# Stick-breaking attention on one Trainium2 core: ScalarE's logarithm of a block put directly behind its exponential, ahead of an older block's weights

## The reference, cut to what matters

```python
def stick_breaking(q, k, v):
    ...
    for blk in range(S // SB_BLOCK):
        ...
        z = jnp.einsum('bthd,bshd->bhts', qf[:, q0:kend], kf[:, :kend]) * scale
        ...
        strict = s_idx < t_idx
        log_beta = jax.nn.log_sigmoid(z)
        log_one_minus = jnp.where(strict, jax.nn.log_sigmoid(-z), 0.0)
        suffix = lax.cumsum(log_one_minus, axis=3, reverse=True) - log_one_minus
        w = jnp.where(strict, jnp.exp(log_beta + suffix), 0.0)
        outs.append(jnp.einsum('bhts,bshd->bthd', w, vf[:, :kend]))
```

## Time and profile before

| | us |
|---|---|
| median of 3 runs | 2780.9 |
| lowest and highest run | 2776.28, 2781.06 |
| the profiled execution's own time | 2779.38 |
| its span, first to last instruction | 2777.6 |
| TensorE busy | 2571.7 (93% of the span) |
| VectorE busy | 1418.5 (51%) |
| ScalarE busy | 1153.7 (42%) |
| GpSimd busy | 378.4 (14%) |
| mean granted TensorE clock | 0.969 |
| the stick-breaking loops, from the first scores to the last product | 1934.4 to 2138.8 |

### The profile page before, as it was taken

One profiled execution on the slowest core, in us unless ns is written; L12 is line 12 of the kernel. 1 busy time (PEld: TensorE's weight loads), 2 busy tenths in 40 slices (PEclk: granted clock), 3 DMA queues, 4 the chain that ended last, 5 costly groups with the idle time before them and its releaser, 6 DMA issues. The chain is left out here.

```text
span 2777.6 us, 38801 instructions
## 1 busy us (share of the span) xinstructions
PE 2571.7 (93%) x14887; PEld 1986.1 (72%) x14887; DVE 1418.5 (51%) x2278; ACT 1153.7 (42%) x1977; POOL 378.4 (14%) x415
## 2 busy tenths in 40 slices
PE   5999999999999999879999999999998999999787
PEld 3778987877778978834337788786334877798776
DVE  5113265666655514666664723421777546265762
ACT  6112344545444321134443622311667647333662
POOL 1000020010020000046752000000000010004710
PEclk8999999999999999989999999999999999998889
DMA  7430000000112131200002220102000221111012
GB/s 265 165 139 23 18 33 1 1 1 1 62 61 91 39 61 46 49 19 1 1 1 91 92 76 31 44 18 76 1 1 23 81 89 32 38 46 61 1 54 76
DMA packets 87992, 139.74 MB, mean 50 GB/s; under 512 B 19513, under 2 KB 54738, under 8 KB 87682
## 3 DMA queue, kind: packets, MB, share of 16 engines
q1 hardware_dynamic: 70592, 75.90, 8.7%
q0 software_dynamic: 16976, 61.30, 6.1%
q10 hardware_dynamic: 242, 0.07, 0.0%
HBM read 120.47 MB, written 16.78 MB: 49 GB/s over the span
## 5 line engine op out<-in xcount | busy, mean ns | idle before, releaser
L169 ACT ACTIVATE WORK<-PS 128x512 f32<-128x512 f32 (+5 forms) x309 | 152.6, 494 | 660.3 <-PE PS L854 388.8
L854 PE MATMUL PS<-HT_R,W_R 128*128 128x512 f32 (+1 forms) x896 | 334.5, 373 | 0.0
L853 PE MATMUL PS<-WORK_R,W_R 128*128 128x512 f32 (+1 forms) x736 | 271.5, 369 | 0.0
L852 PE MATMUL PS<-WORK_R,W_R 128*128 128x512 f32 (+1 forms) x672 | 249.6, 371 | 14.4 <-DVE W_R L169 9.9
L980 PE MATMUL PS<-WORK_R,HT_R 128*128 128x512 f32 x528 | 210.5, 399 | 8.8 <-DVE W_R L169 7.5
L854 PE MATMUL PS<-W_R,WORK_R 128*128 128x256 f32 (+3 forms) x704 | 215.3, 306 | 0.0
L981 PE MATMUL PS<-WORK_R,MIXT_R 128*128 128x512 f32 x544 | 214.6, 394 | 0.0
L169 ACT ACTIVATE HT<-PS 128x1024 f32<-128x1024 f32 (+6 forms) x211 | 156.1, 740 | 135.0 <-PE PS L1288 99.3
L982 PE MATMUL PS<-W_R,HT_R 128*128 128x512 f32 x528 | 207.5, 393 | 0.0
L853 PE MATMUL PS<-W_R,HT_R 128*128 128x256 f32 (+2 forms) x688 | 206.2, 300 | 0.0
L917 PE MATMUL PS<-BASE,WORK 128*128 128x128 f32 (+1 forms) x1186 | 175.0, 283 | 23.7 <-DVE WORK L169 15.1
(11 more groups left out here) (330 smaller groups left out, 5607.2 us busy)
## 6 DMA issues: line engine op xcount, KB each, us to landing
MIXT<-in_w_mod POOLq DMA_DIRECT2D x8, 2048.0 KB, 8.8
x_scratch<-WORK POOLq DMA_DIRECT2D x24, 512.0 KB, 2.9
WORK<-x_scratch POOLq DMA_DIRECT2D x24, 512.0 KB, 3.5
W<-in_odd_w_in SPq DMA_DIRECT2D x12, 1024.0 KB, 5.1
W<-in_even_w_in SPq DMA_DIRECT2D x5, 2048.0 KB, 7.8
W<-in_w_mod SPq DMA_DIRECT2D x4, 2048.0 KB, 21.1
WORK<-in_x POOLq DMA_DIRECT2D x16, 512.0 KB, 8.2
W<-in_e_w_in SPq DMA_DIRECT2D x6, 1024.0 KB, 6.6
```

The lines of the kernel that those rows point to most:

```text
L169: self.last = Signalled(self, issue(*args, **kwargs))
L852: mm(out, a[0], b_[0], start=k == 0, stop=False)
L853: mm(out, a[1], b_[0], start=False, stop=False)
L854: return mm(out, a[0], b_[1], start=False, stop=k == KT - 1)
```

## The change

In ScalarE's loop, iteration n issued exponential n, weights n-2, logarithm n, decay n-2. It now issues exponential n, logarithm n, weights n-2, decay n-2. Nothing else is changed: no instruction, tile, semaphore or wait is added or removed.

```diff
@@ -2114,11 +2114,9 @@
                     e = SE[n % 2][:, :, 0:512 - cols_of(n)]
                     act.wait_ge(low_ready, n + 1)
                     f(e, e, ACT.Exp)
+                    f(e, e, ACT.Ln, bias=1.0).then_inc(ln_ready, 1)
                 if n >= 2:
                     stick_weights(n - 2)
-                if n < len(blocks):
-                    f(e, e, ACT.Ln, bias=1.0).then_inc(ln_ready, 1)
-                if n >= 2:
                     stick_decay(n - 2)
```

## The result

The changed kernel takes 2815.95 us (median of 4 runs, 2814.54 to 2816.87) against 2780.82 (4 runs, 2776.28 to 2781.06): ratio 1.0131, 95% interval 1.0115 to 1.0147, 35.1 us slower. That is the way and within the range forecast, 4.4 us above the 2811.6. The profiled execution took 2815.53 us.

What follows compares the result with a forecast made beforehand. A ring of hand-overs (weights, scores, cap, exponential, weights) bounds the stage. Three periods of 8.25 us make 24.75; with 5.10 ahead and 0.87 and 0.03 behind, about 30.7 us on 2780.9 gives 2811.6 us, range 2802 to 2825.

Steps and rivals of the forecast that it cites:

- The ring: Stick-breaking loops: weights, scores, cap, exponential, next weights wait in turn; the logarithm enters, a 12-block period grows 8.25 us.
- steps 12 and 14: Scores 12 to 13 and 14 to 15: logarithms of 0.66 and 0.45 us hidden wholly in slack under TensorE's own work.
- step 15: Scores 15 to 16: logarithm of 0.87 us, less 0.18 of slack at scores 16.
- step 10: Scores 10 to 11: an older add no longer delays the cap, 0.21 us off the logarithm's cost.
- step 17: Scores 17 to 18: an older add no longer delays the cap, 0.16 us off the logarithm's cost.
- step 18: Scores 18 to 19: an older add no longer delays the cap, 0.14 us off the logarithm's cost.
- step 19: Scores 19 to 20: a decay of 0.60 us leaves the exponential's way, logarithm adds 0.45; TensorE holds scores 20, no growth.
- The clock's case: Rival: TensorE's clock falls in the stage to 0.76, 10 to 59 us beyond the forecast, 2822 to 2870; chance 0.08.
- All logarithms exposed: Rival: slack at TensorE-held starts goes, so all 48 logarithms cost their length, 42 us, 2823; chance 0.04.
- Faster: Rival: logarithm fills ScalarE's wait for sums and the decay goes out earlier; 7.2 us at most, 2773.7; chance 0.03.
- no effect: Rival: the logarithm fits into ScalarE's 50.9 us of idle wherever it stands; chance 0.02.
- Half hidden: Rival: more steps are held by TensorE than modelled, growth only 8 to 20 us, 2795; chance 0.05.

Runs made afterwards that it cites:

- the changed kernel's second run: The changed kernel unaltered, timed again on the same chip as the kernel with fitted repeats: 2818.81 us, ratio 1.0144 to the kernel before.
- Experiment 1: Logarithm taken of the first head only: in the changed kernel 2804.12 us, ratio 1.0087; in the kernel before 2779.78 us, ratio 0.9998.
- experiment 2: Kernel before with weights first, exponential and logarithm side by side: decay last 2772.91 us, ratio 0.9977; decay right behind weights 2766.37 us, ratio 0.995.
- the last kernel of experiment 5: Changed kernel with values computed again in TensorE's idle pieces, without repeats that had not fitted: 2809.77 us, ratio 1.0109 to the kernel before.

## Why the prediction was right, and which term was short

**The ring, and the logarithm in it: shown.** A step with the clock up gives just what was worked out: +0.67 in the step above. A whole period with the clock up is in VectorE's timeline of the changed kernel's second run, caps 32 and 44:

```profile
2096.15 1.22 DVE L169 TENSOR_SCALAR HT<-PS 128x1024 f32<-128x1024 f32 x1 [0.41 <-PE PS L1504]
```

```profile
2154.62 1.23 DVE L169 TENSOR_SCALAR HT<-PS 128x1024 f32<-128x1024 f32 x1 [0.41 <-PE PS L1504]
```

58.47 us, where the forecast said 58.5; the same two caps of the kernel before are 50.32 apart, and the periods that the forecast was made for took 50.25. What the forecast took off for hidden parts was right to 0.1 us in each kind of step where the clock is up: steps 12 and 14 grew by nothing, step 15 by 0.68 (0.69 forecast), step 10 by 0.67 (0.66), step 17 by 0.50 (0.50), step 18 by 0.95 (0.95), and step 19 became 0.10 shorter (0 forecast). The one exception is step 17 in the first period, which grew by 0.79. Experiment 1 shows that the logarithm's own length is paid before the weights and not behind them, experiment 2 that the price goes when the weights stand first.

**Exponential and logarithm do not overlap.** 1.72 us for two of 0.84 in the changed kernel, 2.15 for two of 1.06 before. The Trainium skill's 93 ns of overlap ("ScalarE: Activation LUTs", What ACT_TABLE_LOAD costs) does not show in this in-place pair: each start is about 0.03 us behind the end before it. To go by the row was right.

**Softplus has no taker for an early logarithm:** in the loops no wait of VectorE for ScalarE appears, neither before nor after.

**The term that was missing** is the clock's, put at nothing by a step of that rival: "at the stage's own start TensorE was busy 3.64 of 7 us and the clock stayed at 1.00". I took that as evidence against a fall and left the clock out of the forecast. It was weak evidence: that stretch begins just behind one in which the kernel before did run low, a mean of 0.56 from 1934.39 to 1938.20. In the changed kernel the same stretch and the next one read:

```profile
1939.00:1946.00 7.00, 3.77 (x10) 1.31 (x10) 2.98 (x3) 4.49 (x5) 0.00 (x0) 0.83 0.21 66
1943.70:1950.50 6.80, 6.29 (x12) 2.11 (x14) 2.18 (x2) 2.70 (x4) 0.00 (x0) 0.50 0.00 0
```

The longer step 2 left TensorE idle for 2.64 us before scores 3, where it had been 1.55, and the clock went to its lower level, 1.2 GHz. It did so again in each of the three periods. The same idle pieces do not bring it down every time: in the kernel's second run the third period kept its clock. Here is the same kind of step twice, scores 12 to 13 and, a period later, 24 to 25, in TensorE's timeline of the changed kernel:

```profile
1993.84 1.56 PE L1513 MATMUL PS<-HT 128*128 128x384 f32 x4
1995.33 0.87 PE L1520 MATMUL PS<-HT,ONES 128*64 128x384 f32 x4
...
1996.98 1.13 PE L1504 MATMUL PS<-WORK 64*128 64x512 f32 x4
```

```profile
2052.55 2.61 PE L1513 MATMUL PS<-HT 128*128 128x384 f32 x4
2055.08 1.46 PE L1520 MATMUL PS<-HT,ONES 128*64 128x384 f32 x4
...
2057.33 1.13 PE L1504 MATMUL PS<-WORK 64*128 64x512 f32 x4
```

From 1992.99 the one took 3.99 us to the next scores; from 2051.70 the other took 5.63, with the clock at 0.50 from 2052.9 on. Scores 24 to 25 themselves took 3.98 us in the last kernel of experiment 5, the one with the fitted repeats, where the clock was up.

So the loops' 39.1 us are 30.7 forecast plus 8.4, and the 8.4 go with the low clock. Set beside that kernel, in which the clock stays up after the start, 6.5 us of it stand in five steps: 24 and 36 (1.64 each), 26 (1.52), 41 (0.96) and 10 (0.76). The rest, 1.9 us, is in step 3, which took 6.94 us where 4.21 and a logarithm of 0.87 make 5.08; it lies in the low stretch at the start, which the repeats do not reach.

Against it, 3.0 us came back outside the loops, which the forecast had put at nothing. About 1.5 of them lie behind the loops, where the clock's record has 6.8 us less at the lower level than in the kernel before (85.0 against 91.8). That end took 637.3 us in both runs of the changed kernel, each with 85.0 at the lower level, against 638.8. The other 1.5, ahead of the first cap, did not come again: the second run has its first cap at 1935.80, near the 1936.07 of the kernel before.

So it is partly luck that the whole kernel came within 4.4 us. The loops were 8.4 above their forecast, and the prediction's own sign for that was met: "if the clock in them is under 0.95 the size is wrong", and it was 0.94. The result lies in the upper part of the range, which had been drawn for all logarithms exposed and was filled by the clock. The clock's case had 0.08 and 10 to 59 us on top; it came true in part, with a mean of 0.94 and not 0.76, and cost less than its lower end.

**The rivals.** *All logarithms exposed* (42 us) fell, though the loops' 39.1 us come near it: scores 12 to 13, and the steps like it, still take 3.99 us where the clock is up, as in the kernel before. *Faster* and *no effect* fell with the sign. *Half hidden* fell: scores waited for the weights 42 times for 71.4 us. But the faster rival had its mechanism right for another order: once the weights are the first thing after the sums, ScalarE's wait is for the sums (34.4 us), and exponential, logarithm and decay have their place beside TensorE's work.

## What to carry to other kernels

An engine that idles a third of the time still has places where nothing is free: find the ring of hand-overs that releases the next buffer, and ask of each instruction whether it stands before or behind the hand-over on its engine. Work behind it was hidden here; the same work ahead of it cost its full length at every turn that no other engine held up. Putting the releasing instruction first, ahead of both the exponential and the logarithm, took 13 to 14 us off the kernel before, and 6.8 where a decay was left directly ahead of the next release. When a ring gets longer, count also what the bound engine's new idle pieces do to its clock.

## What the runs showed of the hardware

- A granted clock that was at 1.00 with TensorE busy 46.02 of 50.25 us, in pieces of idle below 1.1 us, fell repeatedly to 0.50 when the pieces grew to as much as 2.2 us at 49.12 of 61.58 busy, though not in every period: from scores 32 to 44 of the changed kernel's second run it stayed at 1.00 with such pieces. The fall made the loops longer by some 8 us out of 242.
- Matmuls repeated in TensorE's idle pieces, writing the same values again, kept that clock up, and the kernel was 9.0 us faster, 6.5 of them in these loops.
- The steps of this pipeline repeat from period to period, and from execution to execution, mostly to 0.02 us as long as the clock does not change (the widest exception is step 17, 4.27 us in the first period and 3.98 later), so that a sum over twelve steps hit 58.47 us with 58.5.
